# Hybrid decoder step: the add into the last state rows ahead of the weight split on VectorE, and two projection steps between the groups of the second inverse round

## The chip, the cores and the metric

One Trainium2 chip (trn2), one of its cores. The metric is the device time of one launch of the kernel in microseconds (us). Of the kernel before, three runs gave 3253.73 us in the median, from 3245.68 to 3255.68 us. One more execution was profiled; all rows below are from it.

## The reference

One layer of a recurrent decoder for 16 + 512 prompt tokens and 8 x 4 sample tokens (560 in all), model width 2048, everything in float32. Cut to what matters here:

```python
h  = rms_norm(x) ; z = h @ w_in             # 2048 -> 6336 + 12304 columns
# branch 1 (RWKV-7), 32 heads of 64, state S[v, k] per head:
for t in tokens:
    sa = S @ a_t
    S  = S * w_t + outer(sa, b_t) + outer(v_t, k_t)
    y_t = S @ r_t
y = (layer_norm(y) * lnx_w + lnx_b + sum(r * k * r_k) * v) * silu(za)
# branch 2 (gated linear attention), 4 heads, chunks of 64 -> ob
m = sigmoid(ga) * y + sigmoid(gb) * ob
x = x + rms_norm(m @ w_out)
# outputs: y_prompt, y_sample, and the states of prompt and samples
```

The recurrence over tokens is computed in chunks of 64 tokens: within a chunk, the effect of the terms `sa` of earlier tokens on later ones is a lower triangular matrix, and what is needed is the inverse of (1 - that matrix).

## The kernel before, in words

The program goes through blocks in turn: it normalises and transposes the input; computes the four heads of branch 2 (up to about 1050 us of the profile); then the 32 heads of branch 1 in 16 **pairs** of heads (two heads of 64 fill the 128 partitions), from about 1050 to 2960 us; and the output projection. This case is about the block of the pairs, `turn_of(i)` for i = 0 to 15, which is written out without a loop. I call them pair 0 to pair 15.

Each engine has its own list of instructions, in the order in which it is written, and semaphores (`Signal` objects) between them. There is no planner: the order is by hand.

**Projections.** For every pair the columns of `w_in` that it needs are multiplied with all 560 tokens, as tiles t = 2 to 7 of 128 columns (t = 6 and 7 are those that the next pair begins with). To keep float32's precision, weights and activations are split in a high and a low part: SyncE loads a tile of weights in two halves of 512 KB (`Projection.load`, line 172), ScalarE rounds it to `w_hi` (`split_hi`, line 181), VectorE subtracts to get `w_lo` (`split_lo`, line 189, two instructions for a tile), and its end lets SyncE load the next tile into `raw`. TensorE then does 32 **steps** for a tile, each of three matmuls of 128 x 128 by 280 columns (lines 203 to 205). `fill` is the list of the steps of tiles 4 to 7, and `run(n)` does the next n of them. They stand between the small matmuls of the heads, as work for TensorE while VectorE and ScalarE turn one small product into the operand of the next.

**The inverse.** There are nine chunks (`NC`), the last of which holds the last 16 prompt tokens and the 32 sample tokens. The inverse is found in rounds. `each(b, left, right, signal)` is one group: for nine chunks and two heads a matmul of 64 x 64 by 64, all into bank b; the profile records 36 matmuls for such a group (52 where `keep=True` also adds an identity), all with line 2061. On TensorE:

- the first round: `each(6, t_d, n_d)`, two steps, then it waits for ScalarE's copies of turned keys (`bk_read`, line 1717) and for `af_ready`, then `each(4, n_d, t_d)`, three steps (lines 2111 to 2118);
- the second round: three groups `each(6, ...)`, `each(4, ...)`, `each(2, ..., inv_mm, keep=True)`, 124 matmuls in a row, then four steps (lines 2123 to 2126). Only the last group signals (`inv_mm`), and the third round waits for `inv_a` and `inv_b`, which ScalarE and VectorE give when they have copied the results.

On VectorE the start of the inverse ends with `inv_ready` (line 1874); then come, one after the other, the subtraction of the identity from `t_full` (line 1876, needed in a later round), the split of weight tile 5 (line 1878), and the add into the last chunk's rows of `af` (line 1880) that gives `af_ready`. The samples' own states enter through that add; it needs ScalarE's second copy into `af` (`af_read`, line 1709). Behind it, for each round, VectorE waits for `inv_mm` and copies out of PSUM (lines 1890, 1892, 1894).

ScalarE's copies of the rounds are line 1721. POOL and SyncE only move data in this block; SyncE's queue holds the weight loads in the order of tiles.

Of the kernel before, what the change touches and what calls it, by code (L numbers as in the profile page):

```python
# [25 lines left out]
MUL, ADD, SUB, MIN, MAX = ALU.mult, ALU.add, ALU.subtract, ALU.min, ALU.max  # L26
ds = bass.ds

P = 128
# [7 lines left out]
C = 64  # L37
NC = 9
NF = 8
# [24 lines left out]
class Signal:  # L64
# [6 lines left out]
    def next(self, i):  # L71

        self.count += 1
        return self.at(i, self.count)
# [16 lines left out]
def build(nc, x_prompt, x_sample, state_rwkv, state_shift, state_gla, meta_tokens, norm_pre, w_in, rwkv_mu, rwkv_w0,  # L91
# [3 lines left out]
    with ctx:  # L95
# [3 lines left out]
        def sig(name, per=0):  # L99
            return Signal(ctx, nc, name, per)  # L100

        psum = ctx.enter_context(nc.psum_tensor("psum", [P, 8, 512], F32))
        bank = [psum[:, n, :] for n in range(8)]
# [44 lines left out]
        def bc(ap, n, axis=1):  # L148

            u = ap.unsqueeze(axis)  # L150
            shape = list(u.shape)
            shape[axis] = n
            return u.to_broadcast(shape)
# [1225 lines left out]
        af = ar(NC, P)  # L1379
# [42 lines left out]
        af_read, af_ready = sig("d_af_read", 2), sig("d_af_ready", 1)  # L1422
# [33 lines left out]
        def pair(b, c, n):  # L1456

            at = 512 + (c - CROSSED) * C
            return psum[:, b:b + 2, :].rearrange("p b x -> p (b x)")[:, at:at + n * C]
# [10 lines left out]
        with nc.Block() as block:  # L1470
# [305 lines left out]
            def _(dve):  # L1776
                i = 0
# [9 lines left out]
                def turn_of(i, last=False):  # L1787
# [3 lines left out]
                    tt, stt, ts = dve.tensor_tensor, dve.scalar_tensor_tensor, dve.tensor_scalar  # L1791
# [81 lines left out]
                    dve.wait_ge(mine.sem, mine.next(i))  # L1873
                    tt(inv[:, CROSSED:NC], n_d[:, CROSSED:NC], bc(eye2, NC - CROSSED), ADD).then_inc(inv_ready.sem, 1)
                    dve.wait_ge(inv_ready.sem, inv_ready.next(i))
                    tt(t_full, t_full, bc(eye2, NC), SUB).then_inc(mine.sem, 1)
                    dve.wait_ge(mine.sem, mine.next(i))
                    pd.split_lo(dve, i, mine, 5)
                    dve.wait_ge(af_read.sem, af_read.at(i, 2))
                    tt(af[:, NF, C:P], af[:, NF, C:P], bank[5][:, 5 * C:6 * C], ADD).then_inc(af_ready.sem, 1)  # L1880
                    dve.wait_ge(af_ready.sem, af_ready.next(i))

                    def both(op, signal):

# [95 lines left out]
                for i in range(NPAIR):  # L1980
                    turn_of(i, last=i == LAST_TURN)

            @block.tensor
            def _(pe):

                def turn_of(i, last=False):
# [43 lines left out]
                    def run(n):  # L2030
                        for _ in range(n):
                            next(fill, None)
# [18 lines left out]
                    def half_of(c, h, crossed):  # L2051
                        return head[1 - h if crossed and c < CROSSED else h]

                    def each(b, left, right, signal=None, crossed=(1, 1), keep=False):

                        for c in CHUNK_ORDER:
                            for identity in ((False, True) if keep and c < CROSSED else (False,)):
                                for h in range(2):
                                    out = pair(b, c, 1)[half_of(c, h, crossed[1])]
                                    at = half_of(c, h, crossed[0])  # L2060
                                    m = mm(out, eye2[at] if identity else left(c)[at], right(c)[at], start=not identity,  # L2061
                                           stop=identity or not keep or c >= CROSSED)
                        if signal:
                            m.then_inc(signal.sem, 1)
# [57 lines left out]
                    pe.sem_inc(waited.sem, 1)  # L2122
                    each(6, of(t2), of(x2), crossed=(0, 1))
                    each(4, of(x2), of(t2), crossed=(0, 1))
                    each(2, of(t2), of(inv), inv_mm, crossed=(0, 1), keep=True)
                    run(4)
                    pe.wait_ge(inv_a.sem, inv_a.at(i, 2))
                    pe.sem_inc(waited.sem, 1)
                    pe.wait_ge(inv_b.sem, inv_b.at(i, 3))
# [115 lines left out]
                for i in range(NPAIR):  # L2245
                    turn_of(i, last=i == LAST_TURN)
# [208 lines left out]
```

## Time and profile before

| | |
|---|---|
| median of three runs | 3253.73 us |
| the profiled execution's own time | 3255.16 us |
| its span | 3253.6 us |
| TensorE matmuls | 3017.0 us, 93% of the span, 33815 matmuls |
| VectorE | 1736.9 us, 53% |
| ScalarE | 1057.7 us, 33% |
| POOL | 400.3 us, 12% |
| mean granted TensorE clock | 0.967 of full |
| from 1050 to 2960 us (the pairs): TensorE | 1847.40 of 1910.00 us, clock 0.99 |

A row of a timeline gives the start of a run of like instructions in us from the span's start, how long they took together, engine, line, operation, the tiles and shapes, and how many they are (x36); in brackets, how long the engine had been idle before, and what ended that. PE is TensorE's matmul, PEld its weight load, DVE VectorE, ACT ScalarE. "issue" means that the engine waited for nothing that the profile shows. Ends of matmuls are modelled, so that rows of TensorE overlap a little; starts are the safer numbers.

### The profile page before, as it was taken

The page shows a single profiled execution, that of the slowest core. Times are in us where ns is not written, and L with a number is a line of the kernel's source. Part 1 is how long each engine was busy: PE and PEld are TensorE (multiplying, and loading weights), DVE is VectorE, ACT ScalarE, POOL GpSimd, SP SyncE. Part 2 cuts the span into 40 slices and gives each one's busy share as a digit, 9 for nine tenths or more (in the row PEclk, how much of TensorE's full clock was granted, in tenths as well). Part 3 has the DMA queues.
Part 4 walks back from the last instruction along what each step waited for, and adds up shares of the span by engine and source line. Part 5 has one row for each costly group of instructions (what it writes and reads, how often), then busy time and mean ns, then how long its engine had stood idle before and what let it go on. Part 6 is the DMA issues. An engine that isn't in the chain of part 4 may idle for free. (4 is left out here: it accounts for less than half of the span.)

```text
span 3253.6 us, 79535 instructions
## 1 busy us (share of the span) xinstructions
PE 3017.0 (93%) x33815; PEld 2771.8 (85%) x33815; DVE 1736.9 (53%) x2561; ACT 1057.7 (33%) x1686; POOL 400.3 (12%) x804
## 2 busy tenths in 40 slices
PE   4899999999997899999999999999999999994995
PEld 3898897997985898899899899899899899893995
DVE  3264454444544564665565565565566565464224
ACT  4332332331431243243243243243243243242222
POOL 2200101001003121021021021021022022011000
PEclk7999999999998999999999999999999999996998
DMA  3323423324324222232132132132122122223322
GB/s 94 98 66 89 154 65 122 108 66 130 99 59 130 57 74 56 61 81 63 47 81 67 42 81 68 42 81 69 50 73 68 46 76 68 54 55 135 88 77 97
DMA packets 368528, 255.11 MB, mean 78 GB/s; under 512 B 19412, under 2 KB 347600, under 8 KB 366288
## 3 DMA queue, kind: packets, MB, share of 16 engines
q1 hardware_dynamic: 342592, 184.18, 20.7%
q0 software_dynamic: 25600, 66.02, 6.5%
q8 instruction: 264, 4.33, 0.6%
q14 instruction: 72, 0.59, 0.1%
HBM read 212.69 MB, written 37.45 MB: 77 GB/s over the span
## 5 line engine op out<-in xcount | busy, mean ns | idle before, releaser
L203 PE MATMUL psum<-act_hi,w_hi 128*128 128x280 f32 (+2 forms) x5184 | 1591.1, 307 | 59.0 <-DVE w_lo L189 41.2
L205 PE MATMUL psum<-act_hi,w_lo 128*128 128x280 f32 (+2 forms) x5184 | 1519.7, 293 | 0.4 <-issue 0.4
L204 PE MATMUL psum<-act_lo,w_hi 128*128 128x280 f32 (+2 forms) x5184 | 1518.2, 293 | 0.0
L203 PEld LDWEIGHTS psum<-act_hi,w_hi 128*128 128x128 f32 (+1 forms) x5184 | 984.8, 190 | 133.6 <-issue 93.7
L204 PEld LDWEIGHTS psum<-act_lo,w_hi 128*128 128x128 f32 (+1 forms) x5184 | 984.7, 190 | 4.5 <-issue 1.0
L205 PEld LDWEIGHTS psum<-act_hi,w_lo 128*128 128x128 f32 (+1 forms) x5184 | 984.6, 190 | 0.6 <-issue 0.6
L189 DVE TENSOR_TENSOR w_lo<-raw,w_hi 128x1024 fp32r<-128x1024 f32 (+1 forms) x324 | 396.2, 1223 | 243.7 <-ACT w_hi L181 231.6
L181 ACT CAST w_hi<-raw 128x1024 fp32r<-128x1024 f32 (+1 forms) x324 | 339.3, 1047 | 41.8 <-DMA raw<-in_w_in_dram 15.0
L1619 POOL DMA_DIRECT2D out_s_rwkv_dram<-arena x128 | 77.7, 615 | 1436.2 <-ACT arena L1758 1436.2
L2061 PE MATMUL psum<-arena 64*64 64x64 f32 x9984 | 210.2, 225 | 45.6 <-DVE arena L1880 27.2
L2061 PEld LDWEIGHTS psum<-arena 64*64 64x64 f32 x9984 | 185.2, 135 | 74.9 <-issue 74.6
L1690 ACT ACTIVATE arena<-psum 128x280 f32<-128x280 f32 x96 | 39.0, 407 | 309.7 <-PE psum L205 308.3
L1721 ACT COPY arena<-psum 128x576 f32<-128x576 f32 x80 | 51.3, 642 | 236.4 <-PE psum L2061 235.9
L416 ACT COPY arena<-psum 128x248 f32<-128x248 f32 (+1 forms) x50 | 18.4, 368 | 262.2 <-PE psum L205 262.1
L1941 DVE SCALAR_TENSOR_TENSOR arena<-psum,arena 128x64 f32<-128x64 f32 x128 | 36.3, 284 | 115.1 <-PE psum L2198 115.0
L728 ACT COPY arena<-psum 128x280 f32<-128x280 f32 x48 | 18.9, 393 | 241.8 <-PE psum L205 241.7
L2382 DVE COPY arena<-psum 128x256 f32 (+1 forms) x32 | 13.6, 425 | 147.8 <-PE psum L2428 147.8
L1585 POOL DMA_DIRECT2D arena<-in_state_rwkv_dram x128 | 74.8, 598 | 44.0 <-DMA m_dram<-arena 38.7
L1966 DVE RECIPROCAL arena<-arena 128x560 f32<-128x560 f32 x16 | 58.4, 3653 | 38.0 <-ACT arena L1765 38.0
L779 ACT ACTIVATE arena<-psum 128x280 f32<-128x280 f32 x32 | 13.0, 405 | 195.8 <-PE psum L205 195.8
L1020 DVE SCALAR_TENSOR_TENSOR arena<-arena,psum 128x512 f32<-128x512 f32 x64 | 47.9, 748 | 51.4 <-PE psum L1317 49.4
L686 POOL DMA_DIRECT2D out_s_gla_dram<-arena x32 | 23.3, 729 | 417.7 <-DVE arena L1020 417.7
(330 smaller groups left out, 3364.7 us busy)
## 6 DMA issues: line engine op xcount, KB each, us to landing
raw<-in_w_in_dram SPq DMA_DIRECT2D x288, 512.0 KB, 4.4
arena<-in_state_gla_dram POOLq DMA_DIRECT2D x32, 512.0 KB, 5.1
out_s_gla_dram<-arena POOLq DMA_DIRECT2D x32, 512.0 KB, 3.3
raw<-in_w_out_dram SPq DMA_DIRECT2D x32, 512.0 KB, 4.4
ob_dram<-arena POOLq DMA_DIRECT2D x16, 280.0 KB, 3.2
arena<-ob_dram POOLq DMA_DIRECT2D x16, 280.0 KB, 4.8
m_dram<-arena POOLq DMA_DIRECT2D x16, 280.0 KB, 2.6
arena<-m_dram SPq DMA_DIRECT2D x4, 1120.0 KB, 12.0
```

Of the source, the lines that this page charges most:

```text
L181: nc.scalar.copy(w_hi[t % 2][:, ks, 0:width], raw[half][:, :, 0:width]).then_inc(self.hi.sem, 1)
L189: eng.tensor_tensor(w_lo[t % 2][:, ks, 0:width], raw[half][:, :, 0:width], w_hi[t % 2][:, ks, 0:width].bitcast(F32), SUB).then_inc(self.lo ...
L203: pe.matmul(out, hi, act_hi[:, k, cols], start=(k == 0), stop=False)
L204: pe.matmul(out, hi, act_lo[:, k, cols], start=False, stop=False)
L205: mm = pe.matmul(out, lo, act_hi[:, k, cols], start=False, stop=(k == KT - 1))
L1020: stt(out=sstate[s % 3][:, n, :], in0=sstate[s % 3][:, n, :], scalar=ends[:, n, GN + s:GN + s + 1], in1=bank[4 + n], op0=MUL, op1=ADD).the ...
L1585: pool.dma_start(state8_in[0:C, s, :].rearrange("v (h k) -> v h k", h=2), state_rwkv[0, s, ds(2 * i, 2)].rearrange("h v k -> v h k")).then ...
L1619: pool.dma_start(s_rwkv[0, s, ds(2 * i, 2)].rearrange("h v k -> v h k"), state_out[0:C, s, :].rearrange("v (h k) -> v h k", h=2)).then_inc ...
L1690: nc.scalar.activation(tg[:, half * HALF:(half + 1) * HALF], bank[half][:, 0:HALF], ACT.Tanh, scale=0.5).then_inc(signal.sem, 1)
L1721: nc.scalar.copy(out, pair(b, 0, NC).rearrange("p (c t) -> p c t", c=NC)).then_inc(signal.sem, 1)
L1966: dve.reciprocal(e_t, e_t).then_inc(mine.sem, 1)
L2061: m = mm(out, eye2[at] if identity else left(c)[at], right(c)[at], start=not identity, stop=identity or not keep or c >= CROSSED)
```

## The change

On VectorE the add that gives `af_ready` now stands ahead of the subtraction from `t_full` and of the split of weight tile 5. On TensorE, of the four projection steps behind the second round's third group, two now stand between its second and its third group.

```diff
@@ -1873,12 +1873,12 @@   (VectorE)
                     dve.wait_ge(mine.sem, mine.next(i))
                     tt(inv[:, CROSSED:NC], n_d[:, CROSSED:NC], bc(eye2, NC - CROSSED), ADD).then_inc(inv_ready.sem, 1)
                     dve.wait_ge(inv_ready.sem, inv_ready.next(i))
-                    tt(t_full, t_full, bc(eye2, NC), SUB).then_inc(mine.sem, 1)
-                    dve.wait_ge(mine.sem, mine.next(i))
-                    pd.split_lo(dve, i, mine, 5)
                     dve.wait_ge(af_read.sem, af_read.at(i, 2))
                     tt(af[:, NF, C:P], af[:, NF, C:P], bank[5][:, 5 * C:6 * C], ADD).then_inc(af_ready.sem, 1)
                     dve.wait_ge(af_ready.sem, af_ready.next(i))
+                    tt(t_full, t_full, bc(eye2, NC), SUB).then_inc(mine.sem, 1)
+                    dve.wait_ge(mine.sem, mine.next(i))
+                    pd.split_lo(dve, i, mine, 5)
 
                     def both(op, signal):
@@ -2122,8 +2122,9 @@   (TensorE)
                     pe.sem_inc(waited.sem, 1)
                     each(6, of(t2), of(x2), crossed=(0, 1))
                     each(4, of(x2), of(t2), crossed=(0, 1))
+                    run(2)
                     each(2, of(t2), of(inv), inv_mm, crossed=(0, 1), keep=True)
-                    run(4)
+                    run(2)
                     pe.wait_ge(inv_a.sem, inv_a.at(i, 2))
                     pe.sem_inc(waited.sem, 1)
                     pe.wait_ge(inv_b.sem, inv_b.at(i, 3))
```

## Rows read from the trace of the kernel before

**Rows 1.** Waits of TensorE, 1077 to 2934 us: total, times, longest.
```profile
PE psum L2061 <- DVE arena L1880: 27.2, 16, 1.7
PE psum L2061 <- issue: 13.9, 26, 2.3
```
**Rows 2.** Timeline, pair 0, from VectorE's subtraction into the second round.
```profile
1094.40 0.76 DVE L1876 TENSOR_TENSOR arena<-arena 128x576 f32<-128x576 f32 x1
...
1094.79 1.51 ACT L1717 COPY arena<-psum 128x512 f32<-128x512 f32 x3 [2.88 <-PE psum L2107]
1095.19 2.48 DVE L189 TENSOR_TENSOR w_lo<-raw,w_hi 128x1024 fp32r<-128x1024 f32 x2
...
1097.71 0.22 DVE L1880 TENSOR_TENSOR arena<-arena,psum 128x64 f32<-128x64 f32 x1
...
1098.08 0.80 PE L2061 MATMUL psum<-arena 64*64 64x64 f32 x36 [1.70 <-DVE arena L1880]
...
1098.98 0.76 DVE L1890 COPY arena<-psum 128x576 f32<-128x576 f32 x1 [1.05 <-PE psum L2061]
...
1100.17 1.03 PE L2061 MATMUL psum<-arena 64*64 64x64 f32 x52
...
1102.69 1.44 PE L2061 MATMUL psum<-arena 64*64 64x64 f32 x72 [1.49 <-issue]
```
**Rows 3.** Timeline, pair 4: first, second and start of third round.
```profile
1579.46 0.80 PE L2061 MATMUL psum<-arena 64*64 64x64 f32 x36 [1.70 <-DVE arena L1880]
...
1581.55 2.26 PE L2061 MATMUL psum<-arena 64*64 64x64 f32 x124
...
1583.96 0.76 DVE L1890 COPY arena<-psum 128x576 f32<-128x576 f32 x1 [2.84 <-PE psum L2061]
...
1585.85 1.33 PE L2061 MATMUL psum<-arena 64*64 64x64 f32 x70 [0.29 <-DVE arena L1894]
```
**Rows 4.** Timeline, pair 0: a group of 52, one of 72, two steps.
```profile
1109.52 1.16 PE L2061 MATMUL psum<-arena 64*64 64x64 f32 x52
...
1110.83 0.43 DVE L1892 COPY arena<-psum 128x256 f32<-128x256 f32 x1 [1.89 <-PE psum L2061]
...
1117.72 1.38 PE L2061 MATMUL psum<-arena 64*64 64x64 f32 x72
1119.03 0.40 PE L203 MATMUL psum<-act_hi,w_hi 128*128 128x280 f32 x1
...
1134.14 0.40 PE L203 MATMUL psum<-act_hi,w_hi 128*128 128x280 f32 x1
...
1135.11 0.33 PE L2198 MATMUL psum<-arena 64*64 64x64 f32 x4
```
**Rows 5.** Timeline, second rounds with a gap: pairs 0, 11 and 15.
```profile
1104.29 0.76 DVE L1890 COPY arena<-psum 128x576 f32<-128x576 f32 x1 [4.54 <-PE psum L2061]
...
2428.23 1.37 PE L2061 MATMUL psum<-arena 64*64 64x64 f32 x42 [2.33 <-issue]
...
2909.72 1.15 PE L2061 MATMUL psum<-arena 64*64 64x64 f32 x58
...
2912.67 0.76 DVE L1890 COPY arena<-psum 128x576 f32<-128x576 f32 x1 [3.37 <-PE psum L2061]
```
**Rows 6.** Windows (us; PE, PEld, DVE, ACT, POOL busy; clock; DMA share; GB/s).
```profile
1339.90:1343.30 3.40, 3.40 (x45) 3.16 (x45) 0.76 (x1) 0.64 (x1) 0.00 (x0) 0.50 0.98 279
...
2428.70:2432.10 3.40, 3.40 (x39) 3.28 (x34) 1.67 (x3) 0.64 (x1) 0.00 (x0) 0.50 0.02 5
```
**Rows 7.** Timeline, pair 2: first round and the copy of the second.
```profile
1339.81 1.31 PE L2061 MATMUL psum<-arena 64*64 64x64 f32 x36 [1.70 <-DVE arena L1880]
...
1345.81 0.76 DVE L1890 COPY arena<-psum 128x576 f32<-128x576 f32 x1 [3.83 <-PE psum L2061]
```
**Rows 8.** Instruction queue: in 1100.3 to 1101.5 us (packets, MB); in the whole span.
```profile
q8 instruction: 1, 0.02, 4.9%
...
q8 instruction: 264, 4.33, 0.6%
```

More of the change, by code:

```diff
@@ L1875, in turn_of @@
                     dve.wait_ge(inv_ready.sem, inv_ready.next(i))
+                    dve.wait_ge(af_read.sem, af_read.at(i, 2))
+                    tt(af[:, NF, C:P], af[:, NF, C:P], bank[5][:, 5 * C:6 * C], ADD).then_inc(af_ready.sem, 1)
+                    dve.wait_ge(af_ready.sem, af_ready.next(i))
                     tt(t_full, t_full, bc(eye2, NC), SUB).then_inc(mine.sem, 1)
@@ L1878, in turn_of @@
                     pd.split_lo(dve, i, mine, 5)
-                    dve.wait_ge(af_read.sem, af_read.at(i, 2))
-                    tt(af[:, NF, C:P], af[:, NF, C:P], bank[5][:, 5 * C:6 * C], ADD).then_inc(af_ready.sem, 1)
-                    dve.wait_ge(af_ready.sem, af_ready.next(i))
                     def both(op, signal):
```

## The prediction

> **What bounds the kernel now.** I read four views. First, what TensorE waited for while the sixteen head pairs run: one cause stands out, the add into the last state rows (L1880), 16 times 1.70 us, 27.2 us in all, and behind it "issue", 13.9 us in 26 places, where no semaphore of the profile was late [rows 1]. Everything else TensorE waits for in that stage is a few us. So TensorE sets the pace there, and an edit is worth what it takes from or adds to TensorE's own sequence. Second, the timeline of pair 0 around those waits [rows 2]: VectorE does the 0.76 us subtraction and the 2.48 us weight split, and only then the 0.22 us add; TensorE has ended its two projection steps 1.70 us before 1098.08 and stands still until then. Third, the same stretch of pair 4, which has no "issue" gap, as the clean pattern [rows 3]. Fourth, the stretches that are longer than the clean one: gaps inside the 124-matmul second round [rows 2, 5], and the clock [rows 6, 7].
>
> **Part 1, the add ahead of the split.** Removed: TensorE's wait. The add may start at 1094.40, where the subtraction started (ScalarE's copy that it needs had long ended: ScalarE was idle 2.88 us before 1094.79), and ends at 1094.62. What is late next is ScalarE's three copies, which end at 1094.79 + 1.51 = 1096.30; a handover costs 0.15 us (add ends 1097.93, TensorE starts 1098.08), so TensorE starts at about 1096.45 instead of 1098.08: 1.63 us earlier [rows 2]. Added: the subtraction and the split now run behind the add, until 1094.62 + 0.03 + 0.76 + 0.03 + 2.48 = 1097.92, and VectorE's copy of the first round (L1890), queued behind them, can start only at 1097.95. The product that it copies is there 0.90 us after TensorE's start (1098.08 to 1098.98), now at 1097.35; so the copy is 0.6 us late, ends at 1098.71, and TensorE restarts at 1098.86. With no such delay it would have been 1100.17 - 1.63 = 1098.54. So 0.32 us of new wait, and 1.31 us won per pair [rows 2]: 16 x 1.31 = 21.0 us. The lower bound of the gain is nothing (if the copy's lateness ate it all), the upper one 1.70 us x 16 = 27.2 us; I take 21.0, as all its terms are rows. The weight split ends 0.25 us later than before, so the next weight load starts 0.25 us later; those weights are needed some 10 us on, behind VectorE's and ScalarE's later split, so I cost that at nothing. The order in which VectorE releases nothing else changes; no DMA is issued by a moved step itself, the loads on SyncE's queue keep their order.
>
> **Part 2, two of four projection steps between the groups.** No instruction is added. The signal of the second round comes only with its third group, and then VectorE's three operations and a handover take 1583.96 to 1585.85 = 1.89 us; today four steps cover all of it but 0.29 us [rows 3]. In the clean pattern the 124 matmuls take 1581.55 to 1583.96 = 2.41 us up to VectorE's start. After: 72 matmuls 1.31 us to the next start, two steps 0.97 us, 52 matmuls 1.31 us to VectorE's start [rows 4], together 3.59 us, 1.18 us more; only two steps are left behind as cover, so TensorE is then idle about 1.1 us instead of 0.29 in each pair. Cost 16 x 1.18 = 18.9 us. Bounds: at least 0.97 - 0.29 = 0.68 us a pair (10.9 us), at most 1.31 us (21 us). What it buys: see the next part.
>
> **The stalls inside the second round.** In pair 0 TensorE stops after 52 of the 124 matmuls for 1.49 us with nothing to wait for [rows 2]. Eight pairs show this, from pair 0 to pair 15 (after 58) [rows 5]; the places are 52, 78, 54, 80, 106, 82, 108 and 58 in pairs 0, 1, 5, 6, 7, 11, 12 and 15: 26 matmuls later from one pair to the next and 2 later after five. With a weight load to each matmul that is one fixed place in every 256 instructions of the stream. And each has a packet of the instruction queue before it: pair 0's is in 1100.3 to 1101.5, in the middle of the next weights' packets, 264 packets in all, 16.4 KB each [rows 8]. So TensorE has run out of instructions: the fetch was asked for late (the queue was held by the wait of part 1) and then lay among the weight load's packets, which set out when the first half of the split has ended (1096.4). From the group's start to VectorE's copy these eight take 4.12 us (pair 0) to 2.95 us (pair 15) instead of 2.41 [rows 2, 3, 5]; the eight excesses sum to 12.9 us.
> After the change TensorE isn't held before the first round, so the fetch is asked for 1.6 us earlier, while the weight load starts 0.25 us later: it should be ahead of the load or among its first packets. Besides, a place beyond the 72nd matmul is reached 0.97 us later behind the two steps, and 0.3 us is added by the late copy. Pair 15, whose fetch met no weight load, shows how short the rest is: 0.54 us of excess [rows 5]. Bounds: all 12.9 us stay, or none; I take 3 us as left, 9.9 us won.
>
> **The clock.** Five stretches of about 3.4 us have TensorE at 0.5 of its full clock, its lower level of 1.2 GHz, in pairs 2, 6, 8, 11 and 13. Four come right after the 1.70 us wait, the one in pair 11 after the 2.33 us stall [rows 6]; gaps up to 1.49 us (pair 0) have drawn none [rows 2]. In pair 2 the stretch from the first round to the copy takes 6.00 us, in pair 4 it takes 4.50 us: 1.50 us each [rows 3, 7]. With the 1.70 us wait and the 2.33 us stall gone, and 1.1 us the longest idle time left, I expect none: three that stand alone give 4.5 us, the ones of pairs 6 and 11 1.3 us beyond what is in the 12.9, and 0.3 us from a short gap in pair 3: 6.1 us.
>
> **Sum.** -21.0 + 18.9 = -2.1; -9.9; -6.1; together -18.1 us. The profiled execution took 3255.2 us (span 3253.6), so 3237.1 us. It was 1.4 us above the median of the runs shown (3253.73, from 3245.68 to 3255.68). I predict 3237 us. The likeliest case's own range is 3229 to 3244.
>
> **Rivals.**
> (a) The gaps stay. The two orders of work balance (-2.1), the clock recovers (-6.1), and the 12.9 us of gaps are no fetch of instructions, or the fetch now meets the later weight load as often as before. For it: other pairs' blocks will lie in other places of the load. Against it: the spacing of 26 matmuls and the packet beside the gap. 3255.2 - 8.2 = 3247 us. Chance 0.18.
> (b) Slower: the new 1.1 us of idle time in front of the third round, in each pair, draws the low clock. It stands behind 52 small matmuls and two steps. A stretch at the low level cost 1.50 us [rows 3, 7]; in all sixteen pairs 24 us, 3237.1 + 24 = 3261 us. From twelve pairs on the gain is gone. For it: four of sixteen waits of 1.70 us did so. Against it: no gap of up to 1.49 us did, and 0.29 + 1.70 us of today falls to 1.1 + 0.3. Chance 0.06.
> (c) The change doesn't do what it says: TensorE's 1.70 us moves whole to the first round's copy, since the 2.48 us split stands ahead of it. Then part 1 gives nothing and part 2 costs 18.9: 3255.2 + 18.9 - 9.9 - 6.1 = 3258 us. Against it: the addition of rows above, which leaves 0.32 us. Chance 0.04.
> Forecast: 0.72.
>
> **Range and chances.** A measurement of this kernel can tell about 0.3% (9.8 us) from no change, that is below 3244 us. The low end is the sum with all gaps gone and the upper bound of part 1, held against the fastest run shown: 3228. The high end takes in rival (a) and the spread of runs: 3250. Faster by over 0.3%: the forecast, and a small part of (a): 0.74. Within 0.3%: most of (a), part of (c) and the upper tail of the forecast: 0.19. Slower: (b) and part of (c): 0.07.
>
> **What would show it.** The wait for L1880 is gone from TensorE's list, with a new one for L1890 of about 0.3 us x 16 in its place; the one for L1894 grows from 0.29 to about 1.1 us per pair. "issue" before L2061 falls from 13.9 us to about 5. The second round shows as 72 matmuls, two steps, 52 matmuls. The clock has no stretch at 0.5 in pairs 0 to 14, or one at most. Wrong: L1890 at over 1 us per pair (c), low-clock stretches behind the L1894 wait (b), gaps of over 1 us in the second round in four pairs or more (a).

## The result, and the profile after

The changed kernel took 3228.83 us in the median of five runs (3224.46 to 3231.71), the kernel before beside it 3252.92 us (3245.68 to 3255.68): 24.1 us less, ratio 0.9936, 95% interval 0.9922 to 0.9951. Predicted were 3237 us, with 3228 to 3250 as the range and 0.74 on faster; the time lies 0.8 us inside the range's lower end and 8 us from its middle figure. The profiled execution took 3224.46 us, its span is 3222.9 us, its mean clock 0.975 (before 0.967).

TensorE's waits in the pairs after the change (engine, line, what it waited for, us in total, times, longest), to be held against [rows 1]:

```profile
PE psum L2061 <- DVE arena L1894: 14.1, 14, 1.1
PE psum L2061 <- issue: 8.2, 34, 0.8
...
PE psum L203 <- issue: 1.8, 1, 1.8
PE psum L205 <- issue: 1.1, 1, 1.1
PE psum L2002 <- ACT arena L1750: 1.0, 1, 1.0
PE psum L204 <- issue: 0.8, 1, 0.8
```

The 27.2 us on the add are gone. In their place stands the wait for VectorE's chain in front of the third round, 1.06 us a pair. The timeline of pair 2 after, against [rows 2, 3]; it begins with the turn of the keys (L2107), from which I count offsets below:

```profile
1324.16 1.15 PE L2107 MATMUL psum<-ident,arena 128*128 128x128 f32 x9
...
1326.08 2.49 DVE L189 TENSOR_TENSOR w_lo<-raw,w_hi 128x1024 fp32r<-128x1024 f32 x2
1327.23 0.80 PE L2061 MATMUL psum<-arena 64*64 64x64 f32 x36 [0.23 <-issue]
1328.60 0.76 DVE L1890 COPY arena<-psum 128x576 f32<-128x576 f32 x1
1329.51 1.38 PE L2061 MATMUL psum<-arena 64*64 64x64 f32 x72
...
1331.79 1.16 PE L2061 MATMUL psum<-arena 64*64 64x64 f32 x52
...
1333.10 0.76 DVE L1890 COPY arena<-psum 128x576 f32<-128x576 f32 x1 [3.75 <-PE psum L2061]
...
1334.99 1.68 PE L2061 MATMUL psum<-arena 64*64 64x64 f32 x88 [1.06 <-DVE arena L1894]
```

The first copy starts right where the split ends (1328.57), as computed: it is late by the split, and TensorE's second round starts 5.35 us after the turn of the keys. From 72 matmuls' start to VectorE's next copy it is 1333.10 - 1329.51 = 3.59 us, and 1.89 us more to the third round. The same offset of the third round is 10.83 us here and, in clean pairs before, 10.94 us (1585.85 [rows 3] less this row of the kernel before):

```profile
1574.91 1.15 PE L2107 MATMUL psum<-ident,arena 128*128 128x128 f32 x9
```

So where nothing else happens, the whole change is worth 0.11 us a pair. The rest comes from what no longer happens. Two windows, the pairs after the change (clock is the number before the DMA share) and the DMA queues in pair 1 after, from its turn of the keys (1205.35) to 1209.72 us; q8 brings instructions, q1 the weights:

```profile
1059.50:2919.00 1859.50, 1828.35 (x25302) 1689.71 (x25300) 1122.34 (x1685) 639.38 (x1000) 261.30 (x516) 1.00 0.24 63
...
q1 hardware_dynamic: 13, 0.01, 2.0%
q8 instruction: 1, 0.02, 1.5%
```

No stretch of the pairs is at half clock any more (five before). The instruction packet of pair 1 starts at 1209.50, 4.15 us after the turn of the keys, and the weight load's first packet 0.12 us behind it (13 by the end of the window); before the change it started at 7.59, in the load, which began at 4.02. Gaps inside the second round are left in pairs 0 (0.38 us), 10 (0.54 us) and 15 (0.25 us). This is pair 10:

```profile
2282.43 1.15 PE L2061 MATMUL psum<-arena 64*64 64x64 f32 x56
2284.12 0.46 PE L2061 MATMUL psum<-arena 64*64 64x64 f32 x16 [0.54 <-issue]
```

The two profiled executions differ by 30.7 us, more than the medians. 7.6 us of that lie ahead of pair 0 (its L2107 starts at 1093.53 and 1085.96), where nothing was changed; over all profiled executions of this document pair 0's L2107 starts anywhere from 1084.6 to 1094.1 us. From pair 0's to pair 15's L2107 the difference is 21.9 us.

### The profile page after: what moved, and what is told of

It is laid out like the page before. It is cut to its first block and busy times, and to the rows that moved or that the text cites. A ratio compares the mean times of both kernels' runs of the same rounds, so it can differ in the third digit from the quotient of the medians.

```text
span 3222.9 us, 79535 instructions
## 1 busy us (share of the span) xinstructions
PE 3006.3 (93%) x33815; PEld 2759.3 (86%) x33815; DVE 1735.9 (54%) x2561; ACT 1056.7 (33%) x1686; POOL 400.2 (12%) x804
## 5 line engine op out<-in xcount | busy, mean ns | idle before, releaser
L2061 PE MATMUL psum<-arena 64*64 64x64 f32 x9984 | 209.4, 223 | 24.3 <-DVE arena L1894 14.1
L2061 PEld LDWEIGHTS psum<-arena 64*64 64x64 f32 x9984 | 184.0, 134 | 55.3 <-issue 55.3
## 6 DMA issues: line engine op xcount, KB each, us to landing
arena<-m_dram SPq DMA_DIRECT2D x4, 1120.0 KB, 12.1
```

## The experiments

Three groups of kernels ran; the kernels of a group shared a chip and the runs of the kernel before (medians 3250.85, 3249.39 and 3255.66 us).

Since the stretch ahead of pair 0 varies by itself, the time from pair 0's to pair 15's L2107 in each profiled execution is given here too. The two kernels that were profiled twice repeat it within 0.8 and 1.9 us.

| kernel | us |
|---|---|
| before | 1809.56 |
| the change | 1787.64, 1786.89 |
| part 1 alone | 1775.51, 1777.40 |
| part 2 alone | 1816.43 |
| stream shifted | 1807.24 |
| load brought forward | 1787.31 |
| load held back | 1811.28 |
| four steps between | 1805.53 |
| copy first | 1778.93 |
| five and three steps | 1785.79 |
| all three | 1777.99 |

**Part 1 alone.**

```diff
-                    tt(t_full, t_full, bc(eye2, NC), SUB).then_inc(mine.sem, 1)
-                    dve.wait_ge(mine.sem, mine.next(i))
-                    pd.split_lo(dve, i, mine, 5)
                     dve.wait_ge(af_read.sem, af_read.at(i, 2))
...
+                    tt(t_full, t_full, bc(eye2, NC), SUB).then_inc(mine.sem, 1)
+                    dve.wait_ge(mine.sem, mine.next(i))
+                    pd.split_lo(dve, i, mine, 5)
```

> Part 1 alone: the add ahead of the subtraction and the split; the four projection steps stay together behind the second round. Theory 1 (the wait in front of the first round went, and with it the late fetch of instructions; the two steps between the groups are a cost): the wait for L1880 is gone as in the changed kernel, the third round starts 1.18 us earlier than there in a clean pair, 16 x 1.18 = 18.9 us; the gaps in the 124-matmul group stay small (0.5 us at most in pairs 0, 10 and 15), but in pairs 3, 8 and 13, where the changed kernel shows 0.8 to 1.8 us of stall behind the group, up to 2 us now fall uncovered, some 6 us. 3228.8 - 18.9 + 6 = about 3216 us (3209 to 3221). Theory 2 (the two steps between the groups are what keeps TensorE supplied with instructions): gaps of 1 to 2 us come back in about eight pairs, 3229 us or more.

Measured: 3217.45 us, ratio 0.9900 (0.9885 to 0.9916), better than both together. In the third group again:

> Part 1 alone once more, as the yardstick for the two others of this group: about 0.990 of the kernel before, 3217 us.

Measured: 3219.89 us, 0.9891 (0.9874 to 0.9907). Its waits and its pair 2 (profile of the first time):

```profile
PE psum L2061 <- issue: 9.6, 36, 1.0
PE psum L2061 <- DVE arena L1894: 4.0, 14, 0.3
...
1333.79 2.26 PE L2061 MATMUL psum<-arena 64*64 64x64 f32 x124
```

The 124 matmuls run through, without the two steps between them. So the steps are not what keeps TensorE supplied: theory 2 falls. No stretch of the pairs is at half clock here either. As theory 1 had it, the third round starts 1.18 us earlier in clean pairs (offset 9.65), and pairs 3, 8 and 13 give some back: 1.49, 0.67 and 0.97 us of "issue" in the steps behind the group, which now have no 1.06 us of idle time to hide in; pairs 4, 9 and 14 show it inside the third round.

**Part 2 alone.**

```diff
+                    run(2)
                     each(2, of(t2), of(inv), inv_mm, crossed=(0, 1), keep=True)
-                    run(4)
+                    run(2)
```

> Part 2 alone: VectorE's order as before, two of the four steps between the second round's groups. Theory 1: the wait for L1880 stays at 27.2 us; each pair pays 1.18 us (18.9 in all); gaps beyond the 72nd matmul (pairs 1, 6, 7, 11, 12) shrink by up to 1 us each, those at 52 to 58 stay; the stretches at half clock stay. 3252.9 + 18.9 - 5 = about 3267 us (3260 to 3272). Theory 2: the gaps in the second round vanish and pay for the steps: 3253 us or less.

Measured: 3266.55 us, ratio 1.0060 (1.0040 to 1.0079): slower than before. The profiled execution was the fastest of the four (3253.08 us), so it says what happens, not where the median's time lies; its pairs took 6.9 us more than before:

```profile
PE psum L2061 <- DVE arena L1880: 27.2, 16, 1.7
PE psum L2061 <- DVE arena L1894: 17.0, 17, 1.1
PE psum L2061 <- issue: 3.5, 18, 0.5
...
1331.40:1334.60 3.20, 3.20 (x77) 2.82 (x76) 0.00 (x0) 0.00 (x0) 0.00 (x0) 0.50 0.54 152
```

The steps do shorten the gaps (13.9 to 3.5 us of "issue"), more than I gave them: with them part 2 has an effect on the supply. But it costs its 1.1 us a pair in front of the third round, and seven pairs are at half clock (2, 4, 7, 9, 10, 12, 14; one window shown), not five. The two parts multiply to 0.9900 x 1.0060 = 0.9959; the change has 0.9936: behind part 1 the second part costs 12 us by these ratios (14 by those of the second and third group below), not 19.5. The interval of part 2 alone goes from 13 to 26 us, so this difference isn't clear of noise.

**The stream of instructions shifted.** The kernel before, with

```diff
+                for _ in range(64):
+                    pe.sem_inc(waited.sem, 1)
+
                 def turn_of(i, last=False):
```

at the head of TensorE's list for the pairs.

> The kernel before with 64 semaphore increments more at the start of TensorE's list for the pairs, nothing else: the stream of instructions is shifted by the place of 32 matmuls with their weight loads. If the gaps are fetches at one place in every 256 instructions, they move by 32 matmuls: 20 instead of 52 in pair 0, 46 instead of 78 in pair 1, 22 in pair 5, 48 in pair 6, 74 in pair 7, or gaps appear in other pairs (places 72 and 98 in pairs 2 and 3). If they come from anything that hangs on the data, the semaphores or how many small matmuls ran in a row, they stay at 52, 78, 54, 80. Time within 10 us of the kernel before.

Measured (one run): 3245.28 us. Second rounds of pairs 2, 3, 7 and 8:

```profile
1332.87 1.38 PE L2064 MATMUL psum<-arena 64*64 64x64 f32 x72
1335.71 1.16 PE L2064 MATMUL psum<-arena 64*64 64x64 f32 x52 [1.46 <-issue]
...
1453.52 1.79 PE L2064 MATMUL psum<-arena 64*64 64x64 f32 x98
1456.65 0.69 PE L2064 MATMUL psum<-arena 64*64 64x64 f32 x26 [1.34 <-issue]
...
1933.82 1.49 PE L2064 MATMUL psum<-arena 64*64 64x64 f32 x74
1936.68 1.16 PE L2064 MATMUL psum<-arena 64*64 64x64 f32 x50 [1.37 <-issue]
...
2054.49 1.79 PE L2064 MATMUL psum<-arena 64*64 64x64 f32 x100
2057.89 0.68 PE L2064 MATMUL psum<-arena 64*64 64x64 f32 x24 [1.60 <-issue]
```

The gaps stand behind 72, 98, 74 and 100 matmuls, in pairs that had none there; pairs 0, 1, 5 and 6 have lost theirs. Pair 7's gap went from 106 to 74 and pair 11's from 82 to 50, 32 matmuls each; at 20, 46, 22 and 48 in pairs 0, 1, 5 and 6, which the expectation also named, none showed. Nothing of data, of what waits for what, or of the number of small matmuls in a row was changed. The gaps are the places where the next block of the stream is missing. How long a block is shows in pair 0 of the copy-first kernel (below), which has a gap in two rounds:

```profile
1091.92 1.03 PE L2062 MATMUL psum<-arena 64*64 64x64 f32 x52
1093.63 1.44 PE L2062 MATMUL psum<-arena 64*64 64x64 f32 x72 [0.68 <-issue]
...
1097.11 0.92 PE L2062 MATMUL psum<-arena 64*64 64x64 f32 x43 [0.28 <-DVE arena L1895]
1098.48 1.08 PE L2062 MATMUL psum<-arena 64*64 64x64 f32 x45 [0.46 <-issue]
```

From gap to gap are 72 + 12 (four steps) + 43 = 127 matmuls, with a weight load each 254 instructions, and the increments behind two waits.

**The weight load brought forward.** Part 1 alone, with the subtraction from `t_full` moved once more, behind the first copy:

```diff
-                    tt(t_full, t_full, bc(eye2, NC), SUB).then_inc(mine.sem, 1)
-                    dve.wait_ge(mine.sem, mine.next(i))
                     pd.split_lo(dve, i, mine, 5)
...
                             both(lambda c, b: dve.tensor_copy((t2, t_d)[n][:, c, :], b(4)), inv_b)
+                        if n == 0:
+                            tt(t_full, t_full, bc(eye2, NC), SUB).then_inc(mine.sem, 1)
+                            dve.wait_ge(mine.sem, mine.next(i))
```

> As part 1 alone, but the subtraction from t_full stands behind the copy of the first round, not ahead of the split: the split and with it the next weight load start 0.79 us earlier, at 3.6 instead of 4.4 us after the turn of the keys, where the fetches stood at 4.2 to 4.3. Theory 1 (the race between fetch and load decides the gaps): the 0.34 us wait for the first round's copy goes (5.4 us), but about nine pairs (0, 1, 2, 6, 7, 10, 11, 12 have their fetch at 4.2 to 4.5) now have it among the load's packets, and gaps of 0.5 to 2 us come back in the second round: 3217 - 5 + 10 = about 3222 us (3214 to 3228). Rival (only TensorE's wait made the fetch late): no gap comes back, 3212 us.

Measured: 3224.04 us, 0.9925 (0.9908 to 0.9942). No semaphore holds TensorE longer than in part 1 alone, but the load's packets start at offset 3.47 instead of 4.27 (counted from the start of L2107; the expectation's offsets of packets are 0.1 us larger, loads and fetches alike). Its waits, pair 1, and the queues there from 1213.3 to 1215.8 us:

```profile
PE psum L2062 <- issue: 18.5, 41, 1.8
...
1214.90 1.50 PE L2062 MATMUL psum<-arena 64*64 64x64 f32 x78
1218.23 1.14 PE L2062 MATMUL psum<-arena 64*64 64x64 f32 x46 [1.84 <-issue]
...
q1 hardware_dynamic: 1246, 0.63, 97.7%
q8 instruction: 1, 0.02, 2.7%
```

Gaps are back in pairs 1, 2, 6, 7, 11 and 12 (1.84, 0.92, 1.56, 0.81, 1.47, 0.78 us), at the places of before (104 in pair 2), with fetches at 5.5 to 6.0 instead of 4.1 to 4.2. An edit that takes wait out of each pair gave 0.9925, where part 1 alone has 0.9900 and 0.9891; these intervals touch, but the pairs took 1787.31 us in the profile against 1775.51 and 1777.40. One stretch at half clock (pair 3, behind a 1.75 us gap) is in it. So the race between fetch and load decides.

**The weight load held back.** The kernel before, with one wait more on SyncE's queue:

```diff
                     for t in range(3, 6 if i == LAST_TURN else 9):
+                        if t == 6:
+                            sp.wait_ge(inv_mm.sem, inv_mm.at(i, 2))
+                            sp.sem_inc(waited.sem, 1)
                         load_rwkv(sp, i, t)
```

> The kernel before; only SyncE's load of weight tile 6 waits in addition until the second round has signalled, so that no weight packets run during the second round. Theory 1 (a late fetch made longer by the weight load's packets): the gaps in the second round fall to 0.6 us at most in every pair, as in pair 15, which has no load; the 1.70 us waits and the stretches at half clock behind them stay, but the one behind the 2.33 us gap goes. Later fetches, some 10 to 14 us after the turn of the keys, meet the held load and may give new gaps in the third and fourth round. About 3244 us (3238 to 3252). Rival (only the wait that holds TensorE makes the fetch late, the load has no part): gaps of 0.9 to 2.3 us stay in pairs 0, 1, 5, 6, 11.

Measured: 3250.44 us, 1.0008 (0.9998 to 1.0017): no change. Pair 1, the waits, and one gap of pair 2:

```profile
PE psum L2064 <- DVE arena L1883: 27.2, 16, 1.7
PE psum L2064 <- issue: 12.7, 17, 1.8
PE psum L204 <- issue: 2.8, 1, 2.8
...
1211.46 2.44 PE L2064 MATMUL psum<-arena 64*64 64x64 f32 x124
...
1340.45 0.40 PE L204 MATMUL psum<-act_lo,w_hi 128*128 128x280 f32 x1 [2.78 <-issue]
```

No second round has a gap, in any of the sixteen pairs, though TensorE was held by the 1.70 us wait as before: the load has its part, the rival falls. The fetches of pairs 6 and 7 came at 5.6 here, where before they lay at 8.1 and 6.4 in the load; so the wait alone doesn't make a gap. What was won came back: the held load met the fetches of the third and fourth round (12.7 us of "issue" again, up to 2.78 us), and eight pairs were at half clock instead of five, five of them behind the 1.70 us wait and three behind later gaps.

**All four steps between the groups.** The changed kernel with `run(4)` ahead of the third group and none behind it.

> The changed kernel with all four steps between the second round's groups and none behind them. Theory 1 (steps behind the last group are the cover of VectorE's 1.89 us chain, steps ahead of it are none; a stretch with some 1.7 us of idle time draws the half clock): the wait for L1894 grows from 1.06 to 1.85 us in each pair, 0.8 x 16 = 12.6 us, and stretches at half clock come back in some pairs (four to eight, 1.5 us each): 3229 + 12.6 + 6 to 12 = 3247 to 3254 us. Theory 2 (it is the supply of instructions that counts, and steps between the groups give it): 3229 us or less.

Measured: 3251.46 us, 1.0010 (0.9999 to 1.0021), the whole gain lost. The changed kernel in the same group:

> The changed kernel itself again, beside the others of this group, as their yardstick: 0.9936 of the kernel before, with one mechanism or the other; about 3230 us.

Measured: 3227.05 us, 0.9933 (0.9916 to 0.9949). Waits of the four-between kernel, its pair 0, and its window at half clock in pair 8:

```profile
PE psum L2061 <- DVE arena L1894: 32.7, 17, 2.0
PE psum L2061 <- issue: 9.7, 34, 1.0
...
1098.84 1.68 PE L2061 MATMUL psum<-arena 64*64 64x64 f32 x88 [2.04 <-DVE arena L1894]
...
2060.00:2066.40 6.40, 5.54 (x99) 5.45 (x100) 1.59 (x4) 1.05 (x2) 0.00 (x0) 0.50 0.01 3
```

The wait grew by 32.7 - 14.1 = 18.6 us, somewhat more than I had (12.6). The clock came otherwise than I had it: of sixteen gaps of 2.04 us, thirteen drew no half clock; it came in pairs 3, 8 and 13, where a late fetch a few matmuls earlier made the idle time 2.7 to 3.0 us together.

**Towards a better version.** The first copy ahead of the split, on top of part 1:

> As part 1 alone, and VectorE's copy of the first round (L1890) also stands ahead of the split of weight tile 5. Theory 1: the remaining 0.34 us of wait in front of the second round goes (5.4 us in all). The next weight load starts some 2.7 us later than in the changed kernel, about 7 us after the turn of the keys: pairs 3, 8 and 13 get their fetch ahead of it (up to 6 us won), but the fetch that all pairs ask for about 8.4 us after the turn of the keys now lies among the load's packets and may cost up to 2 us in some pairs. 3200 to 3215 us, most likely 3208. Theory 2: gaps stay as in part 1 alone: 3224 us or more.

Measured: 3215.04 us, 0.9886 (0.9870 to 0.9903). Against part 1 alone in its group (0.9900) that is no difference clear of the intervals, and the pairs took 1778.93 us against 1775.51; the likeliest figure of the expectation, 3208 us, was missed. Both halves of the expectation are in the trace: the second round starts at offset 5.15 instead of 5.35, and "issue" before its small matmuls is 12.5 us instead of 9.6. Then, on part 1 alone, `run(5)` behind the second and `run(3)` behind the third round:

> Part 1 alone, with five steps behind the second round (0.29 us of wait for L1894 are left there in each pair) and three behind the third (where VectorE's two operations end some 0.4 us before TensorE is through with its four). Theory 1 (cover counts only behind a group that signals): the 0.29 us go in each pair, nothing opens behind the third round beyond 0.1 us: 4 us won, 0.989 of the kernel before, about 3213 us (3209 to 3217). Rival: the third round's chain takes what the second gives, or the shifted steps move no fetch for the better: 3217 us.

Measured: 3219.92 us, 0.9888 (0.9870 to 0.9905), the same as part 1 alone (0.9891). The rival came true, by its second half. Against part 1 alone in its group the wait for L1894 went from 4.0 to 0.2 us; "issue" ahead of L2061 rose from 8.3 us to this, and three stretches came at half clock (pairs 3, 7 and 12), where part 1 alone has none:

```profile
PE psum L2061 <- issue: 13.2, 41, 1.1
PE psum L203 <- issue: 2.8, 1, 2.8
```

And all three together:

> The copy of the first round ahead of the split (as in the copy-first kernel) and the five and three steps together. Theory 1: 0.34 and 0.29 us less wait per pair than part 1 alone, 10 us, of which the later weight load gives back about half in fetch gaps, as measured in the copy-first kernel: 0.9875 of the kernel before, about 3211 us (3205 to 3216). Rival: the gaps give all of it back: 3217 us.

Measured: 3214.81 us, 0.9881 (0.9863 to 0.9899). The intervals of part 1 alone and of these three kernels built on it overlap, at 0.988 to 0.990, all better than the change (0.9933 and 0.9936). None of the three is shown to beat part 1 alone.

## Why the prediction was right, point by point

**Part 1, 1.31 us a pair.** The second round started 6.64 us after the turn of the keys before (1100.17 less 1093.53) and 5.35 after: 1.29 us. One term was off and did no harm: TensorE starts the first round's second group 0.30 us after ScalarE's last copy (pair 0 after: 1087.22 + 1.51 to 1089.03), not 0.15, and the copy that waits for the split swallows that. So the expected 0.32 us came in two places: 0.15 us in the later start of that group, whose idle 0.23 us is listed as "issue" (in pair 0 of part 1 alone, profiled again, as the wait for ScalarE's L1717), and 0.17 us up to the second round, of which 0.11 us is idle time, too short for the list of waits. No wait for L1890 is in it.

**Part 2, 1.18 us a pair.** 3.59 us from the 72 matmuls to the copy and 1.89 behind it, both as computed; 10.83 against 9.65 us with part 1 alone. In time it cost, behind part 1, 12 to 14 us by the medians and 9.5 to 12.1 by the profiled pairs, not the computed 18.9. Up to the third round's start the sixteen pairs take 17.2 us more than with part 1 alone, since the idle time in front of that round covers part of the late fetches of pairs 3, 8 and 13; behind it they take 3.9 us less, 1.9 of them in shorter "issue" gaps, the rest unexplained. What it was to buy, fewer gaps in the second round, it did not buy: with part 1 alone they are 0.26 us at most.

**Gaps and clock, 9.9 and 6.1 us.** Up to the third round the sixteen pairs took 18.96 us more than clean pairs before and 2.7 us more after: 16.3 us against the forecast 16.0. With the clean difference of 1.8 us that is 18.0 us, and the prediction had 18.1. That the fetch gets ahead of the load was right but close: 4.1 to 4.2 in nine pairs against 4.3 for the load in eight of them (pair 15 has none), and a load 0.8 us earlier undid it. The lead is 0.1 to 0.2 us; the prediction left open whether the packet would be ahead or among the load's first, so that it was ahead in all eight was partly luck. The reason that I gave for the clock (the 1.70 us wait and the 2.33 us gap draw it) holds as far as both are gone and so are the stretches; as a rule about the length of one gap it is refuted by the four-between kernel. The kernel before could have shown it: its longest gap without half clock behind it is 1.84 us (pair 1), not the 1.49 us of pair 0 that the prediction took, and twelve of its sixteen waits of 1.70 us drew none.

**What was missing from the sum.** The middle figure, 3237 us, was 8.3 us too high. 2.3 us of that is the start: the sum was taken off the profiled execution's 3255.2 us, and the median before is 3252.92. The rest is in two places. Behind the third round's start the pairs won another 3.5 us (472.8 to 451.3 us from L2107 to L2157, L2158 after, in sixteen pairs, 21.5 in all); "issue" gaps there, as in pairs 7 and 12 before, I had counted as unchanged, and they fell by 2.2 us (5.7 to 3.5). The last 2.6 us between 21.5 and 24.1 lie within the spread of runs, which is 10 us for the kernel before. Two readings of "issue" need care. Ahead of L2061 it is 8.2 us where I had said 5, but 3.6 of these are the sixteen handovers of 0.23 us; in the second round gaps fell from 9.2 us in eight pairs to 1.2 in three. And the gaps that moved to pairs 3, 8 and 13 (1.80, 1.07, 0.81 us) stand ahead of the steps' lines 203, 205 and 204, and aren't in the 8.2.

**The rule on blocks.** The Trainium skill (Runtime: NRT & Kernel Launch, "Instruction fetch mechanics") has blocks of 256 instructions of 16 KiB. The trace agrees, with 127 matmuls and their weight loads between two gaps of one pair; the shift by 64 increments shows that the gaps hang on the place in the stream, as they moved by 32 matmuls. The same section of the Trainium skill says that crossing a block is mostly hidden. In number the trace agrees: the kernel before has 264 packets and 18 "issue" gaps of TensorE over 0.25 us in its whole span. A crossing is not hidden where small matmuls run beside a weight load (1.84 us in pair 1 with the load early, none in the second round with it held), and behind the second round not always ahead of projection steps either (1.80 us at line 203 in pair 3 after).

**Open.** Whether part 2 costs less behind part 1 than alone isn't shown: the intervals overlap, and part 2's profiled execution was the fastest of its four. What decides the half clock beyond the length of a gap wasn't settled. Nor was what exactly holds the request for a block. That TensorE's wait delays it shows in pair 15, which has no load: the packet came at 5.57 before and at 4.08 after. But after the change packets came 4.1 to 4.2 us after the turn of the keys in nine pairs and about 2.0 to 2.1 in four, for places only a few instructions apart.

## What to carry to other kernels

An "issue" gap that wanders by a fixed number of instructions from one pass of unrolled code to the next is a missing block of instructions, and it grows when a large load is started just ahead of the fetch; look at when loads start, not only at what waits for them. Filler work covers a chain only if it stands behind the instruction that releases the chain: the same two steps ahead of it cost at least their whole length (1.18 us for 0.97). Before keeping a change of two parts, time each alone: here one part gave 33 to 36 us and the other cost 12 to 14 of them.

## What the runs showed of the hardware

- TensorE's half clock (its level of 1.2 GHz) does not follow from the longest gap alone: 1.70 us of waiting drew it in 4 (before), 7 (part 2 alone), 5 (load held) and 5 (stream shifted) of 16 pairs, 2.04 us in none of 13. In the changed kernel, with the waits gone, there was none from 1059.5 to 2919 us; but with five and three steps it also came behind gaps of 0.74 and 0.63 us among matmuls of 64 x 4 (pairs 7 and 12, from 1972.3 and 2566.2 us on).
- A packet of 16 KB of the instruction queue that sets out after a weight load of 2 x 512 KB has begun starts 1.3 to 1.9 us later than one that is ahead of it (offsets 5.5 to 6.0 with the load at 3.5, 4.1 to 4.2 with the load at 4.3). Where TensorE stood still for it, it went on 2.3 to 2.9 us after the packet's start.
